# A weight ring of four places and eight u row places, with four units split beside the last gathers

## The reference

```
# first block, two layers
h = h + pool_mixer(rmsnorm(h))                    # layer 0
h = h + o_proj(stick_breaking(q, k, v))           # layer 1: causal, 16 heads of 64
h = h + peer(rmsnorm(h))                          # both layers

def peer(h):                                      # per token: 8 heads x 16 experts = 128
    q = h @ w_query                               # 1024 x 2048
    top 16 of 128 keys in each half, top 16 of the 256 sums, softmax gates
    u_sel, v_sel = u[expert], v[expert]           # rows of two tables of 16384 x 1024
    act = gelu(h . u_sel);  return sum(gate * act * v_sel)

# second block
n = rmsnorm(h)
q_a, k_a, v_a, q_r, k_r, v_r, g_r, q_m, z_a, z_r, z_m = split(n @ w_in)
merged = sigmoid(z_a) * (moba(...) @ w_br_attn) + sigmoid(z_r) * (retention(...) @ w_br_ret)
       + sigmoid(z_m) * (memory_attention(...) @ w_br_mem)
h = h + merged @ w_out
h = h + (gelu(gate) * up) @ w_down                # conv of width 3 over x @ w_up first
return rmsnorm(h)
```

## Time and profile before

| | |
|---|---|
| median of 3 runs | 2038.57 us (2036.56 to 2040.6) |
| the profiled execution | 2036.36 us, span 2034.6 us, mean granted clock 0.982 |
| PE busy | 1774.8 us (87%) |
| DVE busy | 1356.7 us (67%) |
| POOL busy | 1037.5 us (51%) |
| ACT busy | 854.1 us (42%) |
| DMA | 704.27 MB, mean 346 GB/s |
| of it gathers (queue q0) | 553.72 MB |
| of it SP's loads (queue q1) | 147.44 MB |

### The profile page before, as it was taken

How to read it: one execution, slowest core, us unless ns; L and a number is a source line. 1 busy time by engine, 2 the same in 40 slices (tenths; PEclk the granted TensorE clock), 3 DMA queues, 4 the chain that set the end, 5 groups by cost and what they waited for, 6 DMA issues and landing times.

```text
span 2034.6 us, 21815 instructions
## 1 busy us (share of the span) xinstructions
PE 1774.8 (87%) x6507; PEld 1006.1 (49%) x6507; DVE 1356.7 (67%) x2955; ACT 854.1 (42%) x2034; POOL 1037.5 (51%) x1064
## 2 busy tenths in 40 slices
PE   8999777779988897797898977977777999999998
PEld 6655222213344452243545424422222897778997
DVE  4577988556478569846975994454554367578874
ACT  3444434330157133313742444343433455655663
POOL 0767777765567657755775676667775000000000
PEclk9999999999999899998998998999999999999999
DMA  7999999999999999999999999999999554455664
GB/s 282 388 407 408 409 409 409 409 402 388 378 406 383 408 409 409 409 409 400 379 403 409 409 409 409 409 409 406 409 409 388 180 180 139 130 161 175 187 188 136
DMA packets 194308, 704.27 MB, mean 346 GB/s; under 512 B 21624, under 2 KB 23040, under 8 KB 193936
## 3 DMA queue, kind: packets, MB, share of 16 engines
q0 software_dynamic: 152064, 553.72, 68.9%
q1 hardware_dynamic: 40672, 147.44, 21.0%
q10 hardware_dynamic: 1456, 1.72, 0.2%
HBM read 701.60 MB, written 1.06 MB: 345 GB/s over the span
## 4 chain that ended last, share of the span: by engine, by line
PE 41%; DMA 31%; POOL 10%; DVE 8%; issue 6%; ACT 3%; SPq 0%; DVEq 0%; ACTq 0%; POOLq 0%
DMA a<-in_peer_v,eidx 17%; PE ps L967 17%; DMA a<-in_peer_u,eidx 13%; PE ps L678 11%; POOL a L507 5%; POOL a L519 5%; PE ps L584 5%; DVE a L2022 3%; PE ps L701 3%; PE ps L830 2%; DVE ring_r L2209 1%; PE ps L713 1%; PE ps L637 0%; ACT a_r L1608 0%; DVE a L2163 0%
## 5 line engine op out<-in xcount | busy, mean ns | idle before, releaser
L678 PE MATMUL ps<-a,diag 128*128 128x512 f32 (+1 forms) x1880 | 906.1, 614 | 210.5 <-DMA a<-in_peer_v,eidx 165.3
L2022 DVE SCALAR_TENSOR_TENSOR a<-a,ps 128x1024 f32<-128x1024 f32 x528 | 641.3, 1219 | 397.0 <-DMA a<-in_peer_u,eidx 373.2
L678 PEld LDWEIGHTS ps<-a,diag 128*128 128x128 f32 (+1 forms) x1880 | 329.5, 189 | 734.6 <-issue 647.7
L507 POOL DMA_INDIRECT a<-in_peer_u,eidx x528 | 518.0, 981 | 317.2 <-DVE a L2022 155.1
L519 POOL DMA_INDIRECT a<-in_peer_v,eidx x528 | 518.6, 982 | 211.5 <-issue 132.7
L1348 ACT ACTIVATE gel<-dots 128x1 f32<-128x1 f32 x528 | 104.3, 201 | 697.2 <-DVE a L2022 692.0
L967 PE MATMUL ps<-a_r 128*128 128x256 f32 (+1 forms) x1096 | 258.9, 327 | 0.4 <-DVE a_r L2268 0.4
L967 PEld LDWEIGHTS ps<-a_r 128*128 128x128 f32 x1096 | 181.9, 188 | 21.7 <-issue 2.8
L2209 DVE TENSOR_TENSOR ring_r<-wring,a_r 128x1024 fp32r<-128x1024 f32 x95 | 116.0, 1223 | 82.0 <-ACT a_r L1608 81.6
L1360 ACT ACTIVATE diag<-cstc,cga 128x128 f32<-128x128 f32 (+1 forms) x398 | 158.3, 398 | 13.1
L967 PE MATMUL ps<-a_r,ring_r 128*128 128x256 f32 x512 | 142.5, 278 | 0.0
(11 more groups left out here) (301 smaller groups left out, 1783.7 us busy)
## 6 DMA issues: line engine op xcount, KB each, us to landing
wring<-in_units SPq DMA_DIRECT2D x246, 512.0 KB, 4.5
a<-in_peer_u,eidx POOLq DMA_INDIRECT x528, 13.0
a<-in_peer_v,eidx POOLq DMA_INDIRECT x528, 13.1
late<-in_units SPq DMA_DIRECT2D x8, 512.0 KB, 15.6
a<-in_units SPq DMA_DIRECT2D x7, 512.0 KB, 14.7
a<-in_poolm SPq DMA_DIRECT2D x1, 1632.0 KB, 8.5
late<-in_cs SPq DMA_DIRECT2D x1, 1280.0 KB, 8.0
h<-in_xin SPq DMA_DIRECT2D x2, 512.0 KB, 4.3
```

Of the source, the lines that this page charges most:

```text
L507: g.indirect_dma_start(ug[:, n % NU, :], None, peer_u, bass.IndirectOffsetOnAxis(ap=eidx[:, t, k:k + 1], axis=0))\
L678: last = nc.tensor.matmul(ps[0:P, b + j, :], diag[:, pe_slots[n] % ND, 0:P], vg[:, k % NV, j * 512:(j + 1) * 512], start=False, stop=n == ...
L2022: v.scalar_tensor_tensor(ug[:, n % NU, :], ug[:, n % NU, :], 1.0, ps2(0) if t == 2 else ps2(4), ALU.mult, ALU.mult, accum_out=dots[:, k % ...
```

## The change

`R` goes from 6 to 4 and `NU` from 6 to 8, so `wring` loses 8 KB on each partition and `a1` gains as much. `AHEAD` goes from 6 to 4, with slots 62, 74, 86 and 98; the units 4 and 5 of in_v are split and used like the ones after them. The tables (L447, L448) are asked for at unit `SPLIT0` + 8 instead of `SPLIT0` + 12, which follows from `R` and `AHEAD`.

```diff
--- before.py
+++ after.py
@@ -20,8 +20,8 @@
 FFC = DFF // 128
 RET_DK = 128
 
-R = 6
-NU = 6
+R = 4
+NU = 8
 NV = 8
 ND = 6
 TURNS = 9
@@ -53,8 +53,8 @@
 SIDE = dict(mem=3, memT=6, mem_k=9, mem_v=22, trev=36, n2=42, n2T=46, x=49, flip=56)
 
 
-AHEAD = 6
-AHEAD_AT = (62, 70, 78, 86, 94, 102)
+AHEAD = 4
+AHEAD_AT = (62, 74, 86, 98)
 
 
 
@@ -1125,7 +1125,7 @@
                     pe.wait_ge(S("x_low"), X_PARTS["n2B"] + 2)
                 used(ahead(i, 1))
             owe("vr_ev", 2, 0, 1)
-            for u in range(2, 4):
+            for u in range(4):
                 split_halves_unit(u, (4, 5))
             owe("gr_ev", 2, 4, 5)
             for u in range(4):
@@ -1597,7 +1597,7 @@
             def high_places(n):
                 if n >= WIDE0:
                     return 2 * WH
-                return WH if n >= SPLIT0 + AHEAD + WH else AHEAD
+                return WH
 
             def w_high(n):
 
@@ -1671,9 +1671,10 @@
 
                     nc.scalar.activation(vtok[:, k, t, :], ps[:, b0 + t, :], func).then_inc(S(sem), 1)
 
-            w_high(SPLIT0 + 6)
+            for i in (4, 5):
+                w_high(SPLIT0 + i)
             in_v(1, "vr", 0, "vr_ev")
-            for i in (7, 8, 9):
+            for i in (6, 7, 8, 9):
                 w_high(SPLIT0 + i)
             in_v(2, "gr", 4, "sg", ACT.Sigmoid)
             for i in (10, 11, 12, 13):
@@ -2303,7 +2304,7 @@
             y4 = hn[:, 0, :].rearrange("p (t d) -> p t d", t=2)
             mu = tsb[:, 8:16]
             var = tsb[:, 16:24]
-            for i in (6, 7, 8, 9):
+            for i in (4, 5, 6, 7, 8, 9):
                 w_low(SPLIT0 + i)
             for t in range(2):
                 dve.wait_ge(S("sg"), t + 1)
```

## The result

The change makes the kernel slower by 2.1%: 2082.77 us (2079.35 to 2085.1, four runs) against 2039.20 (2036.56 to 2040.6, four runs), a ratio of 1.021 with a 95% interval of 1.0195 to 1.0224. The forecast was 2065 us, with a range from 2054 to 2078. The sign was right, the size was not: 27 us were forecast, 44 came, and 2082.8 lies above the range.

A forecast was written before the change was run, and what follows sets the result against it. Gathers were taken as bound by bytes at 409 GB/s, the weights behind them by PE. Terms 5.1 - 5 + 1 + 1 + 23 + 2 = +27.1 gave 2065 us, range 2054 to 2078.

The forecast's parts named there:

- Step 3: Four ring places beside the gathers: third query pair 3.8 us late, mostly covered by gathers already issued; +1 us (0 to 4).
- step 4: The last gathers' end: PE waits 1.7 us for the fifth unit, tables stay hidden; +1 us (0 to 2).
- steps 5 and 6: Branches and output: loads wait for places, +23 us (20 to 27); PE's clock after two new waits, +2 (0 to 5).
- step 7: Up and down stages: four places refill in time, with 1.7 us left per cycle; 0 us.
- Step 1: Startup: six loads move into the byte-bound gathers, two leave at their end; net +5.1 us (+2.6 to +7.7).
- Step 2: Eight u places: POOL waits less for dots, recovering DMA rate in busy gather stretches; -5 us (0 to -11).
- POOL's issue bound: Rival, chance 0.12: POOL's own 1.39 us per gather limits busy stretches, so more u places give nothing; 2070 us.
- faster: Rival, chance 0.04: six u places limit the DMA rate, so eight lift it throughout the gathers; 2028 us.
- the hidden tail: Rival, chance 0.04: the change does less in the tail, loads come just in time; 2040 us.
- Up and down become load bound: Rival, chance 0.10: DVE's queue exceeds the slack by 0.3 us per cycle over 66 units, 19 us more; 2084 us.

The follow-up runs named there:

- e5: The changed kernel with zero matmuls (24, 12 and 28) filling PE's waits in the tail; 2079.11 us.
- e2: The changed kernel with six places in both rings again, still splitting four units beside the last gathers; 2039.68 us, ratio 1.0005 to the kernel before.
- e13: The changed kernel with six ring places again from vr0 on, the two new ones being v places free after the last sum; 2048.41 us.
- e3: The changed kernel with the tail's splits on ACT and DVE queued behind the gates, turns and norm that don't need them; 2065.98 us.
- e1: The changed kernel with six u places instead of eight, keeping the ring of four and four split units; 2088.33 us.
- e6: The changed kernel with one more slot of sums between the second and third pair of query units; 2076.51 us.
- e8: The changed kernel with tail splits reordered, early loads ahead of the ring, the slot between query pairs, and zero matmuls (4, 4 and 12); 2058.35 us.
- e14: The changed kernel with six ring places from vr0 on, early loads ahead of the ring and the slot between query pairs; 2038.89 us.
- e15: e14 with seven u and nine v places instead of eight and eight; 2038.06 us.
- e9: The same code as e13, on a chip where the kernel before takes 2145.41 us; ratio 1.0100 to the kernel before there.

## Why the prediction was right or wrong

**Step 3 failed.** "Gathers already issued go on meanwhile, so I take 1 of a possible 0 to 4": the delay was right (3.8 us forecast, 4.29 on the row), the cover was not. POOL waited 11.5 us for a v place behind that stand. It issues u and v in turn, so u gathers stopped too, and 16 gathers in flight are 20 us of DMA at most (an estimate, 16 x 1.28); at 1140 to 1160 the rate fell to 301 GB/s. Beside the startup (5.9 us, less 2.5 at 1220) and the u places (-5.6) the ring of four costs the gather phase 11.9 - 3.4 + 5.6 = 14 us by this pair of profiles, and 7 at the least if e5's is taken for the kernel after and e2's for the one before. The term was 1, with a bound of 4. Some 6 us of it are the query pairs, by experiment. The rest no run took apart; in the layer before, a kept unit in `late` came 3.97 us late where before it was 0.89, and the rate at 720 to 740 was 380 instead of 409 GB/s.

**How far each step reaches.** In the pair of profiles 21.0 us are missing from the forecast: 10.8 in the gather phase (11.9 for 1.1), 3.0 in step 4, 5.6 in steps 5 and 6, 1.6 in step 7. Step 3 is the largest: it misses by 13 there, and steps 1 and 2 make up for 2.3. But the gather phase alone doesn't put the time out of the range (2065 + 10.8 = 2076), nor does what lies behind it (2065 + 10.2 = 2075); together they do. By the medians, 17.8 us missing, the gather phase has some 8 and the rest 10. The range was also drawn too narrow for its own steps. It was built from the bounds of steps 2, 5 and 6; those of steps 1, 3 and 4 reach 2.6, 3 and 1 us above what was taken, which would have put its end near 2084.

**Steps 5 and 6 were right in kind and small in size.** The chain came place by place: the first L1053 11.9 us late against the branches where 9.7 was said, the second 16.5 for 12.0 (L1053 rows less 15.9), `add_half` 31.0 for 23.1. With the clock held, the tail up to `up` costs 25.9 for 23, inside the bounds of 20 to 27; the clock is 2 to 5 for 2, inside its bound of 5. It was costed by two new waits. But it fell behind four, of 2.02 (matmuls of 0.63 us instead of 0.39 behind it), 7.16, 4.15 and 8.29 us. That the places are the cause of the chain is shown by e13, that the queues' order makes about half of it by e3.

**Step 4**: +4.0 for +1. The wait for the fifth unit came as worked out (2.05 us, 1.7 said). Left out were the clock behind it, and the tables, said to stay hidden: in the run with six places, where the fifth unit costs nothing, 2.4 us are lost behind them.

**Step 1 was right in kind, and inside its bounds.** The six loads shift the gathers by 5.9 us at 120 to 400, where 7.7 was worked out, and the credit came as said: at 1220 the shift falls by 2.5 us, where the last two loads go missing. Net that is 3.4 for 5.1. **Step 2 was right in kind**, and -5.6 for -5 in size, as well as four runs can tell. The Trainium skill (GPSIMD Engine Reference, section 1, Specifications) says that GpSimd and VectorE contend for an SBUF interface when a VectorE instruction has two inputs in SBUF, as the dot has; the prediction drew from it a rival by which depth would change nothing there. That isn't the limit here: at 600 to 660 383 GB/s became 404. POOL's gathers did stay slow in that stretch, 1.066 and 1.025 us against 1.088 and 1.062; the DMA was full all the same.

**Step 7**: +1.6 for 0. The slack held but for that; there is no gap at each fourth unit.

**The rivals.** POOL's issue bound fell with the 404 GB/s at 600 to 660, which e1 took back to 380; faster fell with 409 GB/s, the hidden tail with the ACT rows. "Up and down become load bound" gave a time near the one measured, 2084, by a mechanism that was not there: those stages lost 1.6 us.

## What to carry to other kernels

A ring's depth is not one number: count the places each stage holds at the same time, and the loads that stand behind a wait in the same queue. Here the gathers can live with four places, once the early loads go first and the third pair comes a slot later, and the stage behind them needs six; places that the first stage frees can be the second one's, and that brought 34 of the 44 us back with the queues as they were. When two rings are issued from one queue in turn, a stall that fills one stops the other too, so a wait of PE is only hidden as long as the shorter ring and the transfers in flight last; and PE's clock behind the wait belongs to its price. And 12 us of a phase in one pair of profiles are not 12 us of cause: here two profiles of the same code lay 5 us apart.

## What was not expected of the hardware

- The clock falls behind short waits, and the length of the wait alone doesn't tell whether it will. The 16 matmuls of L830 take 3.62 us at full clock. After 4.29 us of waiting they took 6.32; after 2.53 and 2.62 us (e6 and e8) 3.69; after 2.57 and 2.55 us (e14 and e15) 5.38. After waits of 7.16 and 4.15 us the eight transposes of L1053 took 1.97 us instead of 1.04. Filled with zero matmuls down to waits of 1.71 and 1.74 us, they took 1.09.
- One chip moved 375 GB/s in the gathers (e9's profile) instead of 409, and the whole execution took 5% longer, the kernel before from 2128 to 2157 us over 23 runs. Weights behind the gathers came at full speed. The same change cost 0.42% (0.27 to 0.58) on one chip and 1.0% (0.46 to 1.55) on that one; the intervals overlap, so that its price differs isn't shown.
